# Output projection of the first mixer: a new order behind the scores

## What is computed

```
for l in 0, 1:
    hn = rms_norm(x, norm_mix[l])
    x = x + (even_mixer if l == 0 else odd_mixer)(hn)
    x = x + hier_moe(rms_norm(x, norm_ffn[l]))
return rms_norm(x, norm_final)

even_mixer(h):
    a_q, a_f, a_i, a_g, b_q, b_k, b_v, b_low, b_r = split(h @ w_in)
    f = lb + (1 - lb) * sigmoid(a_f)
    o_a = chunked_gla(a_q, 1 - f, a_i, log f)            # 4 heads of 128
    y_a = head_norm(o_a) * silu(a_g)
    log_alpha = log_sigmoid(b_low @ w_up + b_up) / 16
    o_b = chunked_gla(b_q / 8, b_k, b_v, log_alpha)      # 4 heads, keys 64, values 128
    y_b = head_norm(o_b) * silu(b_r)
    return concat(y_a, y_b) @ w_out
```

## Time and profile before

| | before |
|---|---|
| timed, median of 3 | 1203.23 us (1202.84 to 1204.14) |
| profiled execution | 1196.82 us |
| its span | 1195.0 us |
| PE, matmul busy | 882.9 us (74%) |
| DVE busy | 348.6 us (29%) |
| ACT busy | 303.2 us (25%) |
| DMA | 442.69 MB, mean 370 GB/s |
| chain that ended last, by engine | DMA 51%, PE 36%, DVE 7%, ACT 3%, issue 2% |

### The profile page before, as it was taken

One profiled execution on the slowest core, in us unless ns is written; L12 is line 12 of the kernel. 1 busy time (PEld: TensorE's weight loads), 2 busy tenths in 40 slices (PEclk: granted clock), 3 DMA queues, 4 the chain that ended last, 5 costly groups with the idle time before them and its releaser, 6 DMA issues.

```text
span 1195.0 us, 25057 instructions
## 1 busy us (share of the span) xinstructions
PE 882.9 (74%) x10181; PEld 539.1 (45%) x10186; DVE 348.6 (29%) x837; ACT 303.2 (25%) x512; POOL 13.2 (1%) x17
## 2 busy tenths in 40 slices
PE   8999697776666666667669998777666666666664
PEld 6988563443333333333338885334333333333332
DVE  5698562111111111111116884111111111111112
ACT  5644442121011111012014754112110110111102
POOL 2000000000000000000001000000000000000000
PEclk9999899999989989889899999999898888899898
DMA  9634197999999999999996378999999999999994
GB/s 340 242 131 175 55 396 321 429 429 428 428 428 428 429 429 429 428 428 428 429 411 239 142 308 343 376 428 429 427 429 428 429 428 428 428 427 430 429 427 200
DMA packets 44818, 442.69 MB, mean 370 GB/s; under 512 B 3616, under 2 KB 4784, under 8 KB 20080
## 3 DMA queue, kind: packets, MB, share of 16 engines
q1 hardware_dynamic: 44368, 440.90, 88.5%
q10 hardware_dynamic: 288, 1.05, 0.2%
q0 software_dynamic: 128, 0.26, 0.1%
HBM read 441.15 MB, written 1.05 MB: 370 GB/s over the span
## 4 chain that ended last, share of the span: by engine, by line
DMA 51%; PE 36%; DVE 7%; ACT 3%; issue 2%; SPq 1%; DVEq 0%; ACTq 0%
DMA weights<-in_moe_w_dram 51%; PE bank L948 12%; PE bank L590 5%; PE bank L591 5%; PE bank L592 5%; PE bank L957 3%; PE bank L966 2%; PE bank L932 1%; PE bank L755 1%; DVE w_lo L1324 1%; PE bank L784 1%; PE bank L673 1%; ACT w_hi L1059 1%; PE bank L941 1%; DVE gates L1709 1%
## 5 line engine op out<-in xcount | busy, mean ns | idle before, releaser
L948 PE MATMUL bank<-weights,gates 128*32 128x256 f32 x4096 | 289.3, 445 | 136.2 <-DMA weights<-in_moe_w_dram 126.6
L948 PEld LDWEIGHTS bank<-weights,gates 128*32 128x32 f32 x4096 | 148.3, 127 | 261.6 <-DMA weights<-in_moe_w_dram 125.5
L957 PE MATMUL bank<-weights,gates 128*32 128x256 f32 x2048 | 123.8, 382 | 85.9 <-DVE gates L1715 59.3
L1713 DVE TENSOR_TENSOR gates<-gates,bank 128x128 f32<-128x128 f32 x64 | 18.4, 288 | 420.0 <-ACT gates L1001 420.0
L957 PEld LDWEIGHTS bank<-weights,gates 128*32 128x32 f32 x2048 | 62.9, 109 | 146.8 <-issue 85.2
L1001 ACT ACTIVATE gates<-bank 128x128 f32<-128x128 f32 (+1 forms) x68 | 20.0, 296 | 415.2 <-PE bank L948 413.2
L1709 DVE TENSOR_TENSOR gates<-bank,vecs 128x256 f32<-128x256 f32 x64 | 27.2, 425 | 266.2 <-PE bank L941 266.2
L966 PE MATMUL bank<-gates 32*128 32x256 f32 x1024 | 73.3, 400 | 31.2 <-ACT gates L1221 31.2
L1324 DVE TENSOR_TENSOR w_lo<-weights,w_hi 128x2048 fp32r<-128x2048 f32 (+1 forms) x32 | 72.4, 2261 | 32.8 <-ACT w_hi L1059 32.8
L932 PE MATMUL bank<-tok,gates 128*32 128x256 f32 x1024 | 68.5, 385 | 15.7 <-issue 9.9
L966 PEld LDWEIGHTS bank<-gates 32*128 32x128 f32 x1024 | 46.2, 184 | 63.4 <-ACT gates L1221 62.0
(11 more groups left out here) (218 smaller groups left out, 940.0 us busy)
## 6 DMA issues: line engine op xcount, KB each, us to landing
weights<-in_moe_w_dram SPq DMA_DIRECT2D x192, 2048.0 KB, 35.2
weights<-in_even_w_in_dram SPq DMA_DIRECT2D x6, 2048.0 KB, 14.6
weights<-in_odd_w_in_dram SPq DMA_DIRECT2D x5, 2048.0 KB, 21.7
weights<-in_even_w_in_dram SPq DMA_DIRECT2D x2, 1024.0 KB, 9.7
weights<-in_even_w_out_dram SPq DMA_DIRECT2D x1, 2048.0 KB, 7.5
weights<-in_even_w_out_dram SPq DMA_DIRECT2D x2, 1024.0 KB, 4.9
weights<-in_odd_w_out_dram SPq DMA_DIRECT2D x1, 2048.0 KB, 7.4
weights<-in_odd_w_out_dram SPq DMA_DIRECT2D x2, 1024.0 KB, 5.5
```

The source lines that it names most:

```text
L948: ins = pe.matmul(bank[6][PASS * j:PASS * (j + 1), 0:T], got_T[:, k % 2, k // 2, :], up[:, k, :, j * P:(j + 1) * P], start=(k == 0), stop= ...
L957: ins = pe.matmul(bank[7][PASS * q:PASS * (q + 1), T:2 * T], hid_T[:, c, :], down[:, c, q * T:(q + 1) * T], start=(c == 0), stop=(c == Q - 1),
```

## The change

Four things are put in another place, in the first mixer alone; no arithmetic of the output is altered.

PE: step 15 comes straight behind the heads of group A, with the last scores of group B in its middle. The first turning follows, then the heads of group B, step 16, step 17 with the second turning in it, step 18, each waiting for only those y rests that it reads (2, 4, 6, 8).

ACT: the silu of the first gates comes right after the cast of step 15, among the scores, followed by a one-element exponential. After the last exponential comes a one-element square root, then the squares and root of group A, ahead of the cross copies of group B and the cast of step 16. The squares of group B come after the silus of the second gates and the first y scaling, with a one-element square root ahead; the cast of step 17 stands between them and their root.

DVE: softplus and both foldings come in front of the second level of group A. Group A's means and scalings come right behind the last mask, ahead of the rest of step 16. Group B's sums follow group A's y scaling, and the rest of step 17 stands between them and the scalings.

The one-element instructions write a spare column. `act.activation(spare, zeros, fn)` makes the engine load the table of `fn`. The two lines `for l in range(2): fold(l)` go with softplus.

```diff
--- before.py
+++ after.py
@@ -814,27 +814,25 @@
                 pe.wait_ge(cross_kept_A, 1)
                 pe.wait_ge(*proj_kept.at(0, 2))
                 heads(0)
-                scores_B(len(LEVELS) + 1)
+                project(15, lambda: scores_B(len(LEVELS) + 1))
+                pe.wait_ge(*y_ready.at(0, 8))
+                pe.wait_ge(cross_kept_B, 2)
+                turn_y(0, 0, 6)
                 pe.wait_ge(scores_kept_B, 2 * (len(LEVELS) + 1))
-                pe.wait_ge(cross_kept_B, 2)
                 pe.wait_ge(*proj_kept.at(0, 4))
                 heads(1)
-
-                def turn_first():
-                    pe.wait_ge(*y_ready.at(0, 8))
-                    turn_y(0, 0, 6)
 
                 def turn_second():
                     pe.wait_ge(*y_ready.at(0, 16))
                     turn_y(0, 4, 6)
 
-                project(15, turn_first)
+                pe.wait_ge(*y_rest.at(0, 2))
+                project_out(0, 16, first=True, midway=lambda: pe.wait_ge(*proj_kept.at(0, 8)))
                 pe.wait_ge(*y_rest.at(0, 4))
-
-                project_out(0, 16, first=True, midway=lambda: pe.wait_ge(*proj_kept.at(0, 8)))
                 project_out(0, 17, midway=turn_second)
+                pe.wait_ge(*y_rest.at(0, 6))
+                project_out(0, 18)
                 pe.wait_ge(*y_rest.at(0, 8))
-                project_out(0, 18)
                 finish_out(0, 19)
 
             def odd_mixer():
@@ -1121,32 +1119,40 @@
                     round_step(0, 7 + i)
                     if i % 2:
                         keep((i - 3) // 2)
+                act.wait_ge(*proj_kept.at(0, 6))
+                f(gates[:, :, 0:512], gates[:, :, 0:512], ACT.Silu).then_inc(gates_open, 1)
+                act.activation(spare[:, 3:4], zeros[:, 0:1], ACT.Exp)
                 exp_B(len(LEVELS) + 1 - LAG + 1)
                 act.wait_ge(scores_ready_A, 3 + len(LEVELS))
                 act.copy(SA[:, 1024:1536], bank[2][:, :]).then_inc(cross_kept_A, 1)
                 exp_B(len(LEVELS) + 1)
+                act.activation(spare[:, 3:4], zeros[:, 0:1], ACT.Sqrt)
+
+                def square_heads(grp):
+                    for a in range(TT):
+                        b = 2 * a + grp
+                        act.wait_ge(*heads_ready.at(0, 2 * grp + a + 1))
+                        f(work(4608 + 512 * b, 512), bank[b][:, :], ACT.Square).then_inc(heads_squared.sem, 1)
+
+                def root_heads(grp):
+                    act.wait_ge(*heads_mean.at(0, grp + 1))
+                    f(by_group(head_r, grp), by_group(head_ss, grp), ACT.Sqrt).then_inc(heads_root.sem, 1)
+
+                square_heads(0)
+                root_heads(0)
                 for j, (dst, src) in enumerate(((SB[:, 512:768], bank[6][:, 0:256]), (SB[:, 1280:1536], bank[7][:, 0:256]))):
                     act.wait_ge(scores_ready_B, 2 * (len(LEVELS) + 1) + j + 1)
                     act.copy(dst, src).then_inc(cross_kept_B, 1)
                 round_step(0, 16)
-                act.wait_ge(*proj_kept.at(0, 6))
-                f(gates[:, :, 0:512], gates[:, :, 0:512], ACT.Silu).then_inc(gates_open, 1)
-                for grp in range(2):
-                    for a in range(TT):
-                        b = 2 * a + grp
-                        act.wait_ge(*heads_ready.at(0, 2 * grp + a + 1))
-                        f(work(4608 + 512 * b, 512), bank[b][:, :], ACT.Square).then_inc(heads_squared.sem, 1)
-                    if grp == 0:
-                        act.wait_ge(*heads_mean.at(0, 1))
-                        f(by_group(head_r, 0), by_group(head_ss, 0), ACT.Sqrt).then_inc(heads_root.sem, 1)
-                act.wait_ge(*heads_mean.at(0, 2))
-                f(by_group(head_r, 1), by_group(head_ss, 1), ACT.Sqrt).then_inc(heads_root.sem, 1)
-                y_scale(0, 1, 7, vec("even_w"))
                 act.wait_ge(*step_done.at(0, 15))
                 for a in range(TT):
                     f(gates[:, a, 512:1024], bank[4 + a][:, :], ACT.Silu).then_inc(proj_kept.sem, 1)
-                for i in (17, 18):
-                    round_step(0, i)
+                y_scale(0, 1, 7, vec("even_w"))
+                act.activation(spare[:, 3:4], zeros[:, 0:1], ACT.Sqrt)
+                square_heads(1)
+                round_step(0, 17)
+                root_heads(1)
+                round_step(0, 18)
                 y_scale(0, 3, 7, vec("even_w"))
                 round_step(0, 19)
 
@@ -1484,6 +1490,9 @@
                 gap_A(2)
                 rest_step(0, 8)
                 keep_A(0)
+                softplus()
+                for l in range(2):
+                    fold(l)
                 decay_A(2)
                 dve.wait_ge(z_logged, 1)
                 dve.wait_ge(z_set, 2)
@@ -1511,12 +1520,7 @@
                 keep_B(6)
                 decay_B(8)
                 keep_B(7)
-                rest_step(0, 16)
-                softplus()
-                for l in range(2):
-                    fold(l)
-
-                for grp in range(2):
+                def mean_heads(grp):
                     for a in range(TT):
                         b = 2 * a + grp
                         dve.wait_ge(*heads_squared.at(0, 2 * grp + a + 1))
@@ -1525,11 +1529,11 @@
                     dve.wait_ge(vector_step, steps[0])
                     part = by_group(head_ss, grp)
                     ts(part, part, 1.0 / P, EPS, ALU.mult, ALU.add).then_inc(heads_mean.sem, 1)
-                for grp in range(2):
+
+                def norm_heads(grp):
                     dve.wait_ge(*heads_root.at(0, grp + 1))
                     part = by_group(head_r, grp)
                     link(dve.reciprocal(part, part))
-                    dve.wait_ge(gates_open, 1)
                     for a in range(TT):
                         b = 2 * a + grp
                         if grp:
@@ -1538,9 +1542,15 @@
                             y = gates[:, a, grp * 512 + h * P:grp * 512 + (h + 1) * P]
                             stt(y, bank[b][:, h * P:(h + 1) * P], head_r[:, 4 * b + h:4 * b + h + 1], y,
                                 ALU.mult, ALU.mult).then_inc(y_ready.sem, 1)
-                    if grp == 0:
-                        y_scale(0, 0, 6, vec("even_w"))
-                        rest_step(0, 17)
+
+                mean_heads(0)
+                dve.wait_ge(gates_open, 1)
+                norm_heads(0)
+                rest_step(0, 16)
+                y_scale(0, 0, 6, vec("even_w"))
+                mean_heads(1)
+                rest_step(0, 17)
+                norm_heads(1)
                 rest_step(0, 18)
                 y_scale(0, 2, 6, vec("even_w"))
                 rest_step(0, 19)
```

## The result

The changed kernel takes 1190.64 us (median of 4, 1190.32 to 1192.99), the kernel before beside it 1203.68 us (median of 4). The ratio is 0.990, 95% interval 0.988 to 0.992: 13.0 us faster, forecast 12.1. The profiled execution of the changed kernel took 1190.86 us.

What follows compares the result with a forecast made beforehand. The bound was taken as the expert weight stream restarted by the fourth expert's load, behind a chain of engine work. PE's new order starts step 18 at 144.0 instead of 156.16: 12.1 off 1203.23 gives 1191.1, range 1189.7 to 1194.8.

Steps and rivals of the forecast that it cites:

- The path: First layer's end is the fourth expert's load issue at 190.5 plus fixed bytes; earlier time lost comes off one for one.
- Rival 3: Stream tied to the first expert's load: gain 10.3, 1192.9 (chance 0.03); or to something else: no change, 1203.2 (0.03).
- PE's sum: PE's new order from 121.25 at full clock: step 18 starts at 144.0 instead of 156.16, gain 12.1 us.
- the 0.2 that I gave to the restart: On PE, 0.2 us added to steps 15 and 17 for resuming after other work inside them.
- DVE and ACT level with PE: Before step 18, both come 0.3 to 0.4 us ahead of PE four times, 0.1 behind once; loss 0 to 1.
- The covers: Work moved into waits among the scores costs 0: 0.8 of DVE's 6.04 us left, 3.8 of ACT's 4.18 used.
- The clock: PE's granted clock is 1.00 from 121 to 156 us, so three matmul groups no longer run at 1.2 GHz.
- The SP queue: First expert's load goes out at about 134.2, moved by 10.3 us; the fourth's at 178.4 instead of 190.49.
- the margin: First expert's 6 MB land in about 15 us, at 149, long before the stream's restart at 178.
- Rival 1: ACT and DVE become the bound, group B's two table loads delaying the chain 2.6 us: gain 9.5, 1193.7; chance 0.17.
- Rival 2: Each ACT table load holds up to 1.28 us longer than its row: gain 7.6, 1195.5; chance 0.04.
- The 6.4 us: Median 1203.23 lies 6.4 above the profiled execution, in a part not placed; the same 12.1 was subtracted from the median.

Runs made afterwards that it cites:

- a_hold: Changed kernel with the first expert's load held on the SP queue until step 17 is done: 1189.60 us.
- a_hold_mix: Changed kernel with the first expert's load held on the SP queue until the end of the mix: 1202.30 us.
- b_warm: Kernel before with 42 matmuls of zeros put into PE's hole, ahead of the wait for the first y: 1201.08 us.
- a_tables: Changed kernel with two more table switches (exponential and square root of one element each) on ACT ahead of group B's squares: 1195.30 us.
- a_silu_back: Changed kernel with the silu of the first gates put back behind the cast of step 16, without the exponential's table load after it: 1197.43 us.
- a_soft_back: Changed kernel with softplus and both foldings put back behind the rest of step 16: 1198.49 us.
- b_same: Kernel before, unchanged, timed and profiled again on the chip that also runs the variants: 1203.60 us.
- b_soft: Kernel before with only softplus and both foldings moved ahead of the second level of group A's scores: 1199.91 us.
- b_soft_warm: Kernel before with softplus and foldings moved among the scores and 24 matmuls of zeros in the hole that is left: 1196.71 us.
- a_best: Changed kernel with step 17's cast moved ahead of y parts and group B's squares, plus nine more zero matmuls before the first projection step: 1191.79 us.
- a_silu_warm: Changed kernel with the silu back behind step 16's cast and 18 matmuls of zeros on PE ahead of the first y wait: 1193.98 us.

## Why the prediction was right

The forecast, 1191.1 and 12.1 us of gain, met 1190.64 and 13.0, and by its own steps:

- **The path.** That the chain ends in a stream whose start is the fourth expert's load: shown, by a_hold and a_hold_mix from both sides. Rival 3 is out.
- **PE's sum.** 144.0 less 118.38 is 25.6 us from the start of the heads to step 18. In the trace after, step 19's first transposes start at 153.91 and 36 matmuls of 0.23 stand ahead of them, so step 18 started at about 145.7, 25.2 behind 120.52. The term was 0.4 too long: the two turnings are 0.87 each, not 1.0, and the 0.2 that I gave to the restart behind another kind of work is not there behind the heads and the second turning (the chain has 0.23 for both first matmuls); the wait of 0.24 takes some of it back. A further 0.3 came from a step 18 that no longer starts behind a wait: 164.63 - 156.16 = 8.5 us for the same 36 matmuls before, 8.2 after. That makes the 12.9 of the stretch out of the forecast 12.1.
- **DVE and ACT level with PE.** I called PE the bound by a hair. Right in its place: one wait, ahead of step 17, forecast 0.1, measured 0.24; but the chain of the changed kernel runs over ACT and DVE there, not over PE. Both sides came 0.5 us sooner after the heads than forecast (PE's work before step 17 done at 18.4 for 18.9, the rest of step 17 at 18.5 for 19.0), so the tie held, with nothing to spare.
- **The covers.** Forecast 0.8 left on DVE and 0.4 on ACT, measured 0.88 and 0.30.
- **The clock.** 1.00 from 121 to 156, and worth 2.0 us of the 12.5 by b_warm.
- **The SP queue.** The first expert's load at 135.96 less 2.1 for the late start is 133.9, forecast 134.2; without effect, as the margin said and a_hold showed. The fourth's at 179.77 less 2.1 is 177.6, forecast 178.4.
- **What was wrong: the price of lateness.** Rival 1 put 2.6 us of lateness at 2.6 us. a_tables, a_silu_back and a_soft_back show 3.0, 4.4 and 5.0 us of added wait at 5.8, 6.9 and 7.6, each followed by matmuls at the 1.2 GHz level; only for a_silu_back is the clock's part separated by a run, for the other two it is read from their windows and rows. Had rival 1 come, it would have cost nearly twice its term, by my estimate about 5 us, or 1196 us, beyond the range's upper end of 1194.8. The forecast did not need the term. My expectations for these three runs repeated the error and all three missed. (Rival 2's sum has a slip of 0.1: 1203.2 less 7.6 is 1195.6.)
- **What I could not place.** The 6.4 us between the profiled execution and the timed runs: they lie in unchanged code behind the stretch, by b_same, and at least in part at places where the clock differs. That I subtracted the gain from the median, and not from that execution, was right for this reason.

## What to carry to other kernels

Look for the instruction from which the bottleneck resource never rests again, and value an edit by how far it moves that instruction; measure it from a fixed instruction ahead of the edit to that one, because unchanged code varied here by 6.5 us, half of the gain. When PE waits for DVE or ACT, price the wait at its length plus the slow matmuls behind it, here 2 to 3 us for waits of 3.2 us and more in this stretch, and nothing for those of 0.2 to 1.2; where it matters, fill the wait with matmuls of zeros in one run and read the difference. And before one instruction is moved ahead on one engine, follow what it delays through the program order of the next engine: a cast moved ahead on ACT cost 0.9 on PE.

## What the runs showed of the hardware

- Beginnings differ, and the clock at the first projection step divides them. In seven of the fourteen profiles (before, b_same, b_soft, b_soft_warm, a_hold, a_hold_mix, a_best) the granted clock is 1.00 from 18 to 21 us, and the heads of group A start between 118.3 and 119.4. In the other seven, the changed kernel's among them, it is 0.50 to 0.61 there, and they start between 120.2 and 120.9. b_same and b_warm have the same code up to there and stand on different sides. So the start alone moves the rest of an execution by 1 to 2.5 us, which no edit here aims at. In the changed kernel's profile the first matmuls run 0.21 apart, in the first profile of the kernel before 0.12. The wait ahead of the first step does not decide it alone: b_soft_warm waited longer than the changed kernel, and stayed at 1.00 (first matmul of the step in the changed kernel and in b_soft_warm, and their windows from 18 to 21).

```profile
17.44 0.55 PE L590 MATMUL bank<-act_hi,w_hi 128*128 128x256 f32 x1 [2.85 <-POOL w_lo L563]
18.00:21.00 3.00, 3.00 (x17) 3.00 (x17) 2.53 (x8) 0.57 (x2) 0.00 (x0) 0.57 1.12 327
```

```profile
17.78 0.36 PE L590 MATMUL bank<-act_hi,w_hi 128*128 128x256 f32 x1 [3.11 <-POOL w_lo L563]
18.00:21.00 3.00, 3.00 (x27) 3.00 (x27) 2.58 (x7) 0.93 (x2) 0.00 (x0) 1.00 1.13 334
```

- Behind the heads, PE had a granted clock of 0.50 after waits of 3.21, 4.39 and 5.03 us, and of 1.00 after waits of 0.24, 0.49 and 1.18.
- Zeros from a bfloat16 tile into a free bank in the place of a wait kept the clock at 1.00, 42 of them in b_warm and 18 in a_silu_warm.
